# Conv border products moved to ScalarE, weight remainders between the weight sums, seven-product blocks at other places

## The reference

```
def conv_glu_ffn(h, w_gate, w_up, conv_w, conv_b, w_down):
    S = h.shape[1]
    g = h @ w_gate
    u = h @ w_up
    gp = jnp.pad(g, ((0, 0), (CONV_WIDTH - 1, 0), (0, 0)))
    g = conv_b + gp[:, 0:S] * conv_w[0]
    for j in range(1, CONV_WIDTH):
        g = g + gp[:, j:j + S] * conv_w[j]
    return (jax.nn.gelu(g, approximate=True) * u) @ w_down
```

## Time and profile before

| | |
|---|---|
| median of three executions | 1419.64 us |
| the profiled execution, whole | 1419.19 us |
| its span in the trace | 1417.4 us |
| TensorE / VectorE / ScalarE / GpSimd busy | 99% / 87% / 58% / 25% |
| granted TensorE clock | 0.999 of full |

### The profile page before, as it was taken

The page is one execution under the profiler, slowest core; times in us unless marked ns, Lnnn a source line. Parts: engine busy times, 40 slices in busy tenths (PEclk is TensorE's granted clock), DMA queues, the critical chain, the costliest instruction groups (busy, mean ns, idle before and its releaser), DMA issues.

```text
span 1417.4 us, 18897 instructions
## 1 busy us (share of the span) xinstructions
PE 1406.1 (99%) x6502; PEld 1172.3 (83%) x6502; DVE 1235.0 (87%) x1867; ACT 822.2 (58%) x1082; POOL 358.5 (25%) x609
## 2 busy tenths in 40 slices
PE   9999999999999999999999999999999999999997
PEld 9888888888878888888888888888888888888886
DVE  6867778975587899989999999999998999999996
ACT  7455544554475656655655655556656666666663
POOL 0702020620003234443324444234444000000000
PEclk9999999999999999999999999999999999999999
DMA  8765656555557677767677776677777576666662
GB/s 265 223 182 158 193 183 192 164 164 178 178 165 242 198 228 238 237 208 228 213 219 240 234 228 208 219 227 224 231 231 240 177 236 212 209 198 210 202 214 93
DMA packets 149706, 293.75 MB, mean 207 GB/s; under 512 B 17232, under 2 KB 30832, under 8 KB 149360
## 3 DMA queue, kind: packets, MB, share of 16 engines
q1 hardware_dynamic: 132416, 274.71, 61.6%
q0 software_dynamic: 16384, 16.81, 4.3%
q10 hardware_dynamic: 816, 1.09, 0.2%
HBM read 273.67 MB, written 2.10 MB: 195 GB/s over the span
## 4 chain that ended last, share of the span: by engine, by line
PE 93%; DVE 4%; DMA 1%; ACT 1%; issue 0%; SPq 0%; POOL 0%; DVEq 0%; ACTq 0%
PE psum L2115 48%; PE psum L1888 7%; PE psum L1892 7%; PE psum L1890 7%; PE psum L2096 5%; PE psum L2098 5%; PE psum L2097 5%; PE psum L1855 3%; DVE w_lo L1595 2%; PE psum L1859 2%; DMA stage<-in_w_qkv 1%; PE psum L1936 0%; DVE up_T L1606 0%; PE psum L1942 0%; ACT w_hi L927 0%
## 5 line engine op out<-in xcount | busy, mean ns | idle before, releaser
L2115 PE MATMUL psum<-w_hi,hT 128*128 128x512 f32 x1696 | 463.4, 389 | 0.0
L2115 PEld LDWEIGHTS psum<-w_hi,hT 128*128 128x128 f32 x1696 | 318.3, 188 | 66.2 <-issue 0.2
L2115 PE MATMUL psum<-w_lo,hT 128*128 128x512 f32 x848 | 261.1, 389 | 0.0
L1125 DVE TENSOR_TENSOR w_lo<-stage,w_hi 128x1024 fp32r<-128x1024 f32 x141 | 175.5, 1250 | 90.0 <-ACT w_hi L657 88.6
L657 ACT CAST w_hi<-stage 128x1024 fp32r<-128x1024 f32 x141 | 147.8, 1051 | 179.3 <-PE psum L1892 142.5
L1595 DVE TENSOR_TENSOR w_lo<-stage,w_hi 128x1024 fp32r<-128x1024 f32 (+1 forms) x198 | 219.4, 1136 | 11.4 <-ACT w_hi L927 11.4
L1097 POOL DMA_DIRECT2D gate_rows_f<-gate_T x256 | 134.8, 536 | 368.4 <-DVE gate_T L1472 315.6
L927 ACT CAST w_hi<-stage 128x1024 fp32r<-128x1024 f32 (+1 forms) x198 | 190.1, 984 | 57.0 <-PE psum L2115 42.0
L2115 PEld LDWEIGHTS psum<-w_lo,hT 128*128 128x128 f32 x848 | 159.2, 188 | 33.0
L1097 POOL DMA_DIRECT2D up_rows_f<-up_T x256 | 134.6, 534 | 45.4 <-DVE up_T L1472 36.0
L1888 PE MATMUL psum<-w_hi,hT 128*128 128x512 f32 x312 | 124.9, 400 | 0.0
(11 more groups left out here) (256 smaller groups left out, 2584.4 us busy)
## 6 DMA issues: line engine op xcount, KB each, us to landing
stage<-in_w_qkv SPq DMA_DIRECT2D x93, 512.0 KB, 3.7
stage<-in_w_gate SPq DMA_DIRECT2D x88, 512.0 KB, 4.2
stage<-in_w_up SPq DMA_DIRECT2D x88, 512.0 KB, 5.2
stage<-in_w_down SPq DMA_DIRECT2D x84, 512.0 KB, 4.7
stage_wide<-in_w_down SPq DMA_DIRECT2D x42, 512.0 KB, 4.5
stage_early<-in_w_gate SPq DMA_DIRECT2D x40, 512.0 KB, 4.2
stage_early<-in_w_up SPq DMA_DIRECT2D x40, 512.0 KB, 5.2
stage<-in_w_o SPq DMA_DIRECT2D x32, 512.0 KB, 3.9
```

Source lines behind the costliest of these rows:

```text
L1125: nc.vector.tensor_tensor(w_lo[s][:, :], stage[s][:, :], w_hi[s][:, :].bitcast(F32), ALU.subtract).then_inc(s_lo, 1)
L2115: ins = nc.tensor.matmul(c_bank(G, t, c), a[:, j, ROWS[t]], w[slot_of[v]][:, COLS[c]], start=(q == 0 and j == 0 and n == 0), stop=False, s ...
```

## The change

1. **Border products.** For the first tokens of the seven later blocks, the products of taps 1 and 0 are made by ScalarE into small buffers `edge_1` and `edge_0` (`edge_products`, at n = 9, eight instructions of 128x7 and 128x14), and VectorE adds each buffer in one instruction (`add_edges`, at n = 12). VectorE's eight small instructions per chunk are gone.
2. **Order in a seven-product block.** VectorE makes the raw units' low parts between the weight sums: first sum, low part of unit 0 (half), second sum, low part of unit 1, third sum, instead of three sums and then the two low parts. SyncE waits for the sums as well before it loads the stage again.
3. **Places.** Seven-product blocks stand at q = 2 and 5, and in groups 0, 2, 4, 6, 8 and 10 also at q = 3. The sums of the normed rows for the third place are made once, before the loop, into a new buffer `h_sums_early`.
4. **Gating steps.** `turn_up` is at n = 8 (was 7), `conv_tap_2` at n = 8 (was 10), `conv_tap_1` at n = 9 (was 11), `conv_tap_0` at n = 12 (was 13), gelu at n = 14 (was 15). The joint products stay at the end of q = 7.
5. `gated_rows` waits for TensorE's last group from chunk 11 on (was 12). The moves of GpSimd are written as gate, up in one loop; their order is the same.

```
-F_SUMMED = (2, 4)
+F_SUMMED = (2, 5, 3)
+EARLY_GROUPS, ALWAYS = 11, 2
+THREE_IN = (0, 2, 4, 6, 8, 10)
...
-        SUMS_AT = tuple(10 + 2 * x for x in range(len(F_SUMMED)))
-        GATE_ADD_AT, UP_ADD_AT, ACT_SCALE_AT, GATE_TURN_AT, UP_TURN_AT = 1, 2, 3, 3, 7
-        CONV_AT, GATED_AT, ACT_GELU_AT = (10, 11, 13), 15, 15
+        SUMS_AT = tuple(9 + 2 * x for x in range(len(F_SUMMED)))
+        GATE_ADD_AT, UP_ADD_AT, ACT_SCALE_AT, GATE_TURN_AT, UP_TURN_AT = 1, 2, 3, 3, 8
+        CONV_AT, GATED_AT, ACT_GELU_AT, ACT_EDGE_AT = (8, 9, 12), 15, 14, 9
...
+            def edge_products(i):
+
+                wait_from(act, s_edge, 2 * i)
+                for w, e, n in ((1, edge_1, 1), (0, edge_0, 2)):
+                    for j in range(CT):
+                        f = i * CT + j
+                        nc.scalar.activation(e[:, :, j, :], gate_F[:, 0:BLOCKS - 1, j, QUADRANT - n:QUADRANT], ACT.Copy,
+                                             scale=conv_c[:, w, f:f + 1]).then_inc(s_edge_product, 1)
...
-                    add_tap(1, j, i, act_F[:, 1:BLOCKS, j, 0:1], gate_F[:, 0:BLOCKS - 1, j, QUADRANT - 1:QUADRANT],
-                            s_conv_1)
...
+            def add_edges(i):
+
+                dve.wait_ge(s_edge_product, (i + 1) * (2 * CT))
+                for n, e in enumerate((edge_1, edge_0)):
+                    dve.wait_ge((s_conv, s_edge)[n], ((i + 1) * CT, 2 * i + 1)[n])
+                    dst = act_F[:, 1:BLOCKS, :, 0:n + 1]
+                    nc.vector.tensor_tensor(dst, dst, e, ALU.add).then_inc(s_edge, 1)
...
-                if i >= min(RETIRED_AT):
+                if i >= EARLY_GROUPS:
                     dve.wait_ge(s_used, block_used(LASTS[i - 1]))
...
                 weight_sum_13(g)
+                unit_low(g, 0, CHUNK)
                 weight_sum_2(g)
+                unit_low(g, 1)
                 weight_sum_4(g)
...
                     sp.wait_ge(s_lo, unit_taken(stage_before[u]))
+                    if is_ffn_summed(stage_before[u] // 2):
+                        sp.wait_ge(s_w_sum, 3 * sums_before(stage_before[u] // 2) + 3)
```

More of the change, by code:

```diff
@@ L216, in layer_kernel, with h_sums_of @@
             w_lo.append(place(f"w_lo{s}", [P, UNIT], F32R))
+        h_sums_early = place("h_sums_early", [P, 1, 2, 2, SEQ], F32R, at=44 * KIB)
+        def h_sums_of(x):
+            return h_sums[:, x, :, :, :] if x < ALWAYS else h_sums_early[:, x - ALWAYS, :, :, :]
         for s in range(len(EARLY_SLOTS)):
@@ L256, in layer_kernel @@
         table_warm = sb("table_warm", [P, 1])
+        edge_1 = diag[:, 0, 0:(BLOCKS - 1) * CT].rearrange("p (q f c) -> p q f c", q=BLOCKS - 1, f=CT)
+        edge_0 = diag[:, 1, 0:(BLOCKS - 1) * CT * 2].rearrange("p (q f c) -> p q f c", q=BLOCKS - 1, f=CT)
         psum = ctx.enter_context(nc.psum_tensor("psum", [P, 8 * CHUNK], F32))
@@ L356, in layer_kernel @@
         QUADRANT_MOVES = (P // QUADRANT) ** 2
-        s_conv = sem("conv_ready")
+        s_conv = sem("conv_taps_added")
+        s_edge_product = sem("conv_block_edge_products")
+        s_edge = sem("conv_block_edges_added")
         s_gelu = sem("gelu_ready")
@@ L431, in layer_kernel @@
                   + [(F_GROUPS + p, q) for p in range(PASSES) for q in range(PAIRS)])
-        SUMS = (F_SUMMED,) * F_GROUPS + SUMMED
+        SUMS = tuple(tuple(sorted(F_SUMMED)) if G in THREE_IN else F_SUMMED[:ALWAYS] for G in range(F_GROUPS)) + SUMMED
+        JOINT_AT = tuple(blocks.index((G, CHUNK_UNITS - 1)) if G < F_GROUPS
+                         else blocks.index((G, 0)) + SUMS[G][-1] + 3 for G in range(len(SUMS)))
         FIRSTS = [blocks.index((G, 0)) for G in range(len(SUMS))]
@@ L503, in quarters, with is_ffn_summed @@
             return pair_stage(g).rearrange("p (b n) -> p b n", b=4)
+        def is_ffn_summed(g):
+            return 0 <= g < D0 and is_summed(g)
         def w_sum_of(g):
@@ L951, in take_first_product @@
                 if G < F_GROUPS:
-                    act.wait_ge(s_conv, (G + 1) * (2 * CT))
+                    act.wait_ge(s_edge, 2 * (G + 1))
                 nc.scalar.copy(y_of(G, 0, 0), p_bank(G, 0)[:, :]).then_inc(s_p1, 1)
@@ L964, in gating_steps @@
                     conv_tap_2(i)
+                if n == ACT_EDGE_AT:
+                    edge_products(i)
                 if n == ACT_GELU_AT:
@@ L982, in _ @@
                             gating_steps(G, 2 * q + j)
-                if g - 3 in ENDS:
-                    take_first_product(ENDS.index(g - 3))
+                if g in JOINT_AT:
+                    take_first_product(JOINT_AT.index(g))
                 if g == D0 + PAIRS + 3:
@@ L1105, in move_up @@
                 move_quadrants(i, turned[1], up_F, s_up_turned, s_up_F)
-            move_gate(0)
-            for i in range(1, F_ITERS):
-                move_up(i - 1)
+            for i in range(F_ITERS):
                 move_gate(i)
-            move_up(F_ITERS - 1)
+                move_up(i)
             inverse_root_of(0, 6)
@@ L1643, in sums, with sums_and_unit_lows @@
                 nc.vector.tensor_tensor(s4, a12, s2, ALU.subtract).then_inc(s_a_sum, 1)
-            def sums_of_weights(g):
+            def sums_and_unit_lows(g):
                 before = [h for h in range(g) if is_summed(h)]
@@ L1695, in gating_steps @@
                     conv_tap_0(i)
+                    add_edges(i)
                 if n == GATED_AT:
@@ L1713, in _ @@
                         gated_sum_low(g)
+                        unit_low(g, 1)
                     else:
-                        sums_of_weights(g)
-                        unit_low(g, 0, CHUNK)
-                    unit_low(g, 1)
+                        sums_and_unit_lows(g)
                     for n in range(2):
@@ L1726, in _ @@
                             gating_steps(G, 2 * q + j)
-                if g - 3 in ENDS:
-                    joint_products(ENDS.index(g - 3))
+                if g in JOINT_AT:
+                    joint_products(JOINT_AT.index(g))
                 if g == D0 + PAIRS + 2:
@@ L2090, in summed_rows_of @@
                 q = blocks[g][1]
-                return h_sums[:, F_SUMMED.index(q), part, :, :] if g < D0 else (a_hi, a_lo)[part](entry[g] + 1)
+                return h_sums_of(F_SUMMED.index(q))[:, part, :, :] if g < D0 else (a_hi, a_lo)[part](entry[g] + 1)
             def rows_product(o, rows, g, w, cs, j, ts, start):
```

12 lines of the change are left out of this document (5 added, 7 removed).

## The result

The changed kernel takes 1440.82 us (median of 4 runs, 1440.23 to 1441.43); the kernel before took 1419.48 beside it (4 runs, 1419.17 to 1419.71). The ratio is 1.015, interval 1.0133 to 1.0168: slower by about 21 us. The profiled execution took 1440.23 us with a span of 1438.4, against 1419.19 and 1417.4 before.

The account below looks back on a forecast made before the run. TensorE, busy 99%, bounds the kernel before. From 1419.19 us: two-groups +4.8, three-groups +5.4, late groups +9.6, group 0 -0.7, last chunk +0.5, sum +19.6, giving 1438.8 us; range 1425 to 1451.

Parts of the forecast that it names:

- rival (c): Whole kernel: the gain stands, buffers carry VectorE through and tap 2 doesn't hold it; 1415.1 us, chance 8%.
- (a): Gate moves: landings come sooner, at the row's minimum of 1.7 us; +10.7, 1430 us, chance 15%.
- (d): Whole kernel: gain and loss about cancel, VectorE's list 1 us shorter a group; 1417 to 1422 us, chance 5%.
- Rival (b): Gate moves: landings come later in busier queues, each 0.5 us costing 0.5 in 14 groups, +7, 1446 us; chance 12%.
- The chain through tap 2: Gating: tap 2 waits for gate moves landing T + 18.0 (T: group's first matmul), delaying a cast, then 21.9 us of VectorE.
- Two-groups: Groups with two seven-product blocks: loop 0.6 us too long against 42.16; eight ordinary ones cost +4.8 us.
- Three-groups: Groups with three seven-product blocks: period 43.5 us, 1.35 more than before; four ordinary ones cost +5.4 us.
- Late groups: Groups 4 and 11, GpSimd starting gate moves some 2.7 us late: 47.1 us instead of 42.16, together +9.6.
- Group 0 and what is before it: Group 0, gate half turned and moved before the loop: 41.48 us, -0.7; third place's sums before the loop: 0.
- After the loop: Last chunk, gated in the first down pass with VectorE on the path: between -0.5 and +2, taken as +0.5 us.
- Border products: Eight on ScalarE a chunk, 0.3 us each, 2.4 in all, hidden; VectorE's two adds 0.55, net -0.6.
- Waits: ScalarE for gate moves 45 to 50 us in all, VectorE as long for casts, TensorE some 20 for low parts.

Follow-up runs that it names:

- the kernel with the old steps: Changed kernel with seven-product blocks at places 2 and 4 in every group and gating steps numbered as in the kernel before: 1418.24 us, ratio 0.9993.

## Why the prediction was right, point by point

Forecast 1438.8, measured 1440.82, within the range; rival (c), that the gain stands, is refuted, and so are (a) and (d). Rival (b) isn't borne out either: the last move landed 3.2 to 4.0 us after its issue in the ordinary groups, around the 3.7 taken.

- **The chain through tap 2.** Right in place, and in size by two small errors that cancel: in the ordinary two-groups the landing came at 17.6 to 18.2 where 18.0 was said, 0.2 sooner in the mean, and VectorE's list behind it is 22.1 where 21.9 was said. GpSimd starts at T + 6.46 as before, the landing ends the wait, and the group is tap 2's place + 24.95. Shown by undoing it in two ways: moving tap 2 with the steps behind it, and letting the moves land sooner without moving anything, each takes away some 16 us; adding it alone to the kernel before costs 34.6.
- **Two-groups.** +4.8 forecast; the eight are +5.0 over the 42.16 that each took before.
- **Three-groups.** 43.5 forecast, 43.66 measured: +6.0 for +5.4. The reason was right as well: ScalarE's timeline has no wait before tap 2 there, and with early landings they stay as long. The 0.2 that the working took off from 43.7 was right, since the add starts 0.2 behind T; what it lacks is the 0.2 of VectorE's list.
- **Late groups.** They came in groups 4 and 11, at T + 9.19 and 9.18, as in the earlier trace rows. +3.8 and +5.2 for 4.8 each, which agrees in the sum alone; the landing of the last move took 3.92 us in group 4 and 5.33 in group 11. The working's own numbers, 47.1 less 42.16, would have given 4.9.
- **Group 0 and what is before it.** -1.05 for -0.7.
- **After the loop.** 345.3 against 343.2, +2.1, where I took +0.5 from a range that ended at 2. This is the term that was mis-sized most. It was 343.5 with tap 2 one place later and 342.3 with half of the gate moves, so the wait for the landing is in it. With the rows added later it was 345.4 again, so that isn't all; no experiment took it apart.
- **The sum.** 5.0 + 6.0 + 9.0 - 1.05 + 2.1 = 21.05; the spans differ by 21.0.
- **Border products.** 0.3 each was estimated. By line and form they are 294 and 296 ns long, but eight take 1.68 us, 0.2 from start to start, and the two adds on VectorE 0.47 together (0.55 was said):

```profile
L905 ACT ACTIVATE diag<-gate_rows_f,conv_c 128x7 f32<-128x7 f32 x64 | 14.3, 296 | 0.0
```

The difference changed nothing, as the kernel with the old steps shows.

- **Waits.** Forecast some 45 to 50 us before tap 2, nearly as much of VectorE for casts, and some 20 of TensorE for low parts; the list has 45.1, 55.0 for all casts, and 19.4 + 7.1 at the weight loads.
- **The rule on offloading.** The Trainium skill, "Perfetto Trace Analysis", section "Optimizing Scalar/DVE Operations", had it that moving work from a saturated DVE to Scalar may make sense. The move and the new order together took 0.8 us a group from VectorE, measured, and changed nothing that can be told from the spread (0.9993, interval 0.9984 to 1.0002), since TensorE was the bound. So what the page advises brought no gain here.
- **What I had wrong beside the number.** I wrote that no work can be carried over from a light group to a heavy one. It holds with the rows added where the change adds them. With the rows added one step later the pair of groups 2 and 3 closes in TensorE's own time, 83.67. So it was a property of that step, not of the kernel.

Open: the rest after the loop, and why a landing is late now and then: in group 2 of the kernel with two blocks everywhere (44.11 us) GpSimd started at T + 6.46 as ever and the last move took 4.81 us to land, so that tap 2 came at T + 19.16, where its neighbours had it at 18.0 and 17.6.

## What to carry to other kernels

An engine works its list in order, so an instruction that waits for a DMA is priced by what stands behind it: here tap 2 began no sooner when it was moved behind the second cast of q = 4, and still waited for the same DMAs, and the kernel was 15.7 us faster, since the cast (and what VectorE makes from it) no longer stood behind that wait. Ask of every step that is moved earlier whether what it waits for also comes earlier. And read the loop, not the shares: on totals VectorE had room for the third block, and the room lay in one place, which the moved wait used up.

## What the runs showed of the hardware

- In both profiles, of before and after, and in every experiment but the one with half of the gate moves, GpSimd's gate moves start 2.7 us late in groups 4 and 11: before and after at T + 9.18 or 9.19 against 6.46. Counted from VectorE's first add it is 8.99 us against 6.26, and 7.86 against 5.13 with the rows added later. GpSimd's timeline of the changed kernel has four bursts of 16 moves that it began later than anything released it:

```profile
621.08 8.44 POOL L1128 DMA_DIRECT2D gate_rows_f<-gate_T  x16 [26.08 <-issue]
764.37 8.44 POOL L1128 DMA_DIRECT2D up_rows_f<-up_T  x16 [5.29 <-issue]
926.49 8.44 POOL L1128 DMA_DIRECT2D gate_rows_f<-gate_T  x16 [22.66 <-issue]
1071.63 8.44 POOL L1128 DMA_DIRECT2D up_rows_f<-up_T  x16 [6.20 <-issue]
```

  They are seven bursts apart, 112 moves. With 8 gate moves a chunk there are three, all of them bursts of up moves and each five chunks, 120 moves, behind the last. So it seems to go roughly by the number of moves issued. What GpSimd does then, no run shows.
- A wait of TensorE can cost more than itself. Behind a wait of 2.34 us the granted clock was 0.62 over 4.5 us; matmuls ran 0.44 us from start to start in place of 0.227, which is the lower of its two levels (1.2 of 2.4 GHz), and eight of them cost 1.7 us more. It is not every such wait: in the same run TensorE waited as long ahead of group 9, and in group 11 of the changed kernel longer, and both times the clock stayed:

```profile
834.73 0.70 PE L2150 MATMUL psum<-w_hi,hT 128*128 128x512 f32 x2 [2.32 <-DVE w_lo L1628]
...
835.74 1.07 PE L2150 MATMUL psum<-w_hi,hT 128*128 128x512 f32 x4
```

```profile
944.07 0.72 PE L2150 MATMUL psum<-w_hi,hT 128*128 128x512 f32 x2 [2.80 <-DVE w_lo L1628]
...
945.10 1.08 PE L2150 MATMUL psum<-w_hi,hT 128*128 128x512 f32 x4
```
